# Two-layer trunk, convolution stage: two weight slabs split earlier, six taps moved from TensorE to VectorE

## What is computed

```
for i in range(2):
    x = x + 0.5 * swiglu_ffn(rms_norm(x, ffn1_norm[i]), ffn1_w_in[i], ffn1_w_out[i])
    xn = rms_norm(x, mix_norm[i])
    y = pool_conv_mixer(xn, ...) if i == 0 else sgu_mixer(xn, ...)
    x = x + y
    x = x + 0.5 * swiglu_ffn(rms_norm(x, ffn2_norm[i]), ffn2_w_in[i], ffn2_w_out[i])
out = rms_norm(x, final_norm)
```

```
a, gate = split(h)                      # 512 channels each
g = a * sigmoid(gate)
y = causal depthwise conv(g, width 31) + conv_b
return silu(layer_norm(y))              # mean and variance over the 512 channels
```

## Time and profile before

| | before |
|---|---|
| median of 3 runs | 940.22 us (940.21 to 940.26) |
| profiled execution, first to last instruction | 938.5 us |
| around that span, in the median | 1.7 us |
| PE busy | 927.6 us (99%) |
| DVE busy | 522.7 us (56%) |
| ACT busy | 411.9 us (44%) |
| mix0's convolution part, PE's first tap to the mean | 239.7 to 267.0 us |

### The profile page before, as it was taken

One profiled execution on the slowest core, in us unless ns is written; L12 is line 12 of the kernel. 1 busy time (PEld: TensorE's weight loads), 2 busy tenths in 40 slices (PEclk: granted clock), 3 DMA queues, 4 the chain that ended last, 5 costly groups with the idle time before them and its releaser, 6 DMA issues.

```text
span 938.5 us, 15299 instructions
## 1 busy us (share of the span) xinstructions
PE 927.6 (99%) x6505; PEld 872.2 (93%) x6505; DVE 522.7 (56%) x464; ACT 411.9 (44%) x413; POOL 26.7 (3%) x44
## 2 busy tenths in 40 slices
PE   8999999999999999999999999999999999999997
PEld 7999999989989999999999999999999899999995
DVE  5765545446967665455547444554478475454533
ACT  6453334326744544333435344334364265343322
POOL 1500000000000000000000000000010000000000
PEclk9999999999999999999999999999999999999999
DMA  8985555523512875676518656556184277556501
GB/s 264 310 270 179 179 179 201 196 75 120 172 46 101 303 241 180 217 236 202 179 45 278 217 179 213 184 197 190 46 288 161 90 242 263 185 177 209 196 7 45
DMA packets 124213, 170.36 MB, mean 182 GB/s; under 512 B 2773, under 2 KB 108777, under 8 KB 124168
## 3 DMA queue, kind: packets, MB, share of 16 engines
q1 hardware_dynamic: 124168, 169.69, 54.1%
HBM read 168.63 MB, written 1.05 MB: 181 GB/s over the span
## 4 chain that ended last, share of the span: by engine, by line
PE 96%; issue 1%; DVE 1%; DMA 1%; ACT 1%; POOL 0%; SPq 0%; POOLq 0%; ACTq 0%; DVEq 0%
PE ub L894 10%; PE ub L896 10%; PE ub L895 10%; PE ga L894 10%; PE ga L896 10%; PE ga L895 10%; PE acc L894 10%; PE acc L895 10%; PE acc L896 10%; PE ga L1093 1%; PE tp L955 1%; DMA raw<-in_ffn_w_in_dram 1%; PE ub L1093 1%; PE tp L1180 0%; DVE w_lo L607 0%
## 5 line engine op out<-in xcount | busy, mean ns | idle before, releaser
L607 DVE TENSOR_TENSOR w_lo<-raw,w_hi 128x2048 fp32r<-128x2048 f32 (+1 forms) x154 | 352.1, 2295 | 246.3 <-ACT w_hi L410 246.1
L410 ACT ACTIVATE w_hi<-raw 128x2048 fp32r<-128x2048 f32 (+1 forms) x154 | 292.1, 1902 | 91.9 <-PE acc L896 61.5
L894 PE MATMUL ub<-xn_hi,w_hi 128*128 128x256 f32 x688 | 195.1, 284 | 0.0
L894 PE MATMUL ga<-xn_hi,w_hi 128*128 128x256 f32 x688 | 194.8, 283 | 0.2 <-ACT sgh L455 0.2
L896 PE MATMUL ub<-xn_hi,w_lo 128*128 128x256 f32 x688 | 194.7, 283 | 0.0
L895 PE MATMUL ub<-xn_lo,w_hi 128*128 128x256 f32 x688 | 194.7, 283 | 0.0
L896 PE MATMUL ga<-xn_hi,w_lo 128*128 128x256 f32 x688 | 194.7, 283 | 0.0
L895 PE MATMUL ga<-xn_lo,w_hi 128*128 128x256 f32 x688 | 194.7, 283 | 0.0
L894 PE MATMUL acc<-w_hi,act_hi 128*128 128x512 f32 x416 | 163.6, 393 | 0.0
L895 PE MATMUL acc<-w_lo,act_hi 128*128 128x512 f32 x416 | 162.3, 390 | 0.0
L896 PE MATMUL acc<-w_hi,act_lo 128*128 128x512 f32 x416 | 161.9, 389 | 0.0
(11 more groups left out here) (130 smaller groups left out, 766.0 us busy)
## 6 DMA issues: line engine op xcount, KB each, us to landing
raw<-in_ffn_w_in_dram SPq DMA_DIRECT2D x88, 1024.0 KB, 5.1
raw<-in_ffn_w_out_dram SPq DMA_DIRECT2D x44, 1024.0 KB, 5.0
raw<-in_sgu_w_in_dram SPq DMA_DIRECT2D x8, 1024.0 KB, 5.3
raw<-in_ab_w_in_dram SPq DMA_DIRECT2D x6, 1024.0 KB, 4.9
raw<-in_ab_w_out_dram SPq DMA_DIRECT2D x4, 1024.0 KB, 4.8
raw<-in_sgu_w_out_dram SPq DMA_DIRECT2D x4, 1024.0 KB, 7.1
gain<-in_ffn_norm_dram SPq DMA_DIRECT2D x4, 512.0 KB, 5.8
xres<-in_x_dram SPq DMA_DIRECT2D x2, 512.0 KB, 6.3
```

The source lines that it names most:

```text
L410: act.activation(w_hi[:, n % RING, o:], raw[:, n % RAW, o:], ACT.Copy).then_inc(hi_split, 1)
L607: dve.tensor_tensor(w_lo[:, n % RING, o:], raw[:, n % RAW, o:], w_hi[:, n % RING, o:].bitcast(F32), ALU.subtract).then_inc(lo_split, 1)
L894: pe.matmul(dst, s_hi, m_hi, start=start, stop=False)
```

## The change

`SHARED` falls from 16 to 10, so TensorE does the last 10 taps of tile 2 and not 16, ACT builds 41 diagonals and not 47, and DVE does 21 taps of tile 2 and not 15. ACT splits slab b+6 ahead of the first 16 diagonals. DVE splits slabs b+5 and b+6 ahead of the second gate product; the split after q = 8 goes, the ones after q = 12 and 16 are again slabs b+7 and b+8.

```diff
-        SHARED = 16
+        SHARED = 10
         pe_taps = [(CT - 1, q) for q in range(TAPS)] + [(CT - 2, q) for q in range(TAPS - SHARED, TAPS)]
...
                     gate(b + 2, f + 1, ACT.Sigmoid)
+                    split_to(b + 6)
                     act.wait_ge(cols_ready, 1)
                     build_taps(0, DIAGS)
-                    split_to(b + 6)
...
+                    split_to(b + 6)
                     product(b + 3, f + 1, out=conv_in[:, 2:4, LEAD:])
-                    split_to(b + 5)
                     dve.wait_ge(ub_free, f + 2)
                     for q in range(5, TAPS):
 
                         for c in (0, 2, 1) if q - 5 < TAPS - SHARED else (0, 1):
                             tap(c)
 
-                        if q in (8, 12, 16):
-                            split_to(b + 6 + (q - 8) // 4)
+                        if q in (12, 16):
+                            split_to(b + 7 + (q - 12) // 4)
```

## The result

| | before | after |
|---|---|---|
| median of 21 runs | 940.12 us (939.93 to 940.26) | 942.58 us (940.90 to 943.93) |
| ratio of the mean times | | 1.0023, 95% interval 1.0016 to 1.0029 |
| profiled execution, span | 938.5 us | 941.0 us |

The changed kernel is slower, by 0.23% in the mean of its runs and by 2.46 us (0.26%) in the median, and outside my range of 940.5 to 941.8. The runs of after don't scatter, they fall in three groups: 7 runs at 940.90 to 941.09, 11 at 942.34 to 942.79, and 3 at 943.67 to 943.93. The runs of before form one group, 0.3 us wide. The first group of after is my forecast of 941.08; two thirds of the runs are not in it.

What follows compares the result with a forecast made beforehand. TensorE was taken to bound the stage, VectorE 1.2 us behind. Six taps save TensorE 2.59 us, but it must wait for VectorE, so the mean starts 0.86 us later: 940.22 + 0.86 = 941.08 us, range 940.5 to 941.8.

Steps and rivals of the forecast that it cites:

- Parts 1 and 2: Convolution stage: six taps leave TensorE, saving 2.59 us at 0.432 each, and cost VectorE 2.38 us at 0.396 each.
- Parts 3 and 4: Before the second product: early splits leave VectorE 4.2 us less loaded; ScalarE's first 16 diagonals start 1.9 us later, costing nothing.
- The wait at L802: Middle of VectorE's taps: it waits 3.6 us for ScalarE's unmoved high part, so the addition ends at 267.75, 1.92 us later.
- Rival B: TensorE's pause before the mean: its clock falls, costing 1.8 us, at worst twice that; 942.9 to 944.7 us, chance 0.08.
- The new hole is shorter: TensorE's pause before the mean: 3.3 us, against the 4.6 us from stop to clock fall at the kernel's end.

Runs made afterwards that it cites:

- SHARED 8: The changed kernel with SHARED = 8 in place of 10, two more taps on VectorE: 944.40 us median, five runs at 943.47 to 944.49.

## Why the prediction was wrong

Point by point:

- **Parts 1 and 2, the price of a tap on either engine: right.** With the wait out of the way 2.59 us came back, and 22 taps on VectorE took the forecast 8.71 us from start to start (258.51 to 267.22).
- **Parts 3 and 4, the moved splits: right.** Product at 228.43 (228.6 forecast), first tap at 229.15 (229.3), the splits alone change nothing (940.09 against 940.10 us).
- **The wait at L802: right.** 3.53 us (3.6 forecast), addition at 267.22 (267.34), pause 3.30 us (3.3). It holds for the part of the time that it was about: 7 of the 21 runs lie at 940.90 to 941.09, my 941.08.
- **Rival B, the clock: this is the step that failed.** Its price was right (1.8 us forecast and at worst 3.6; measured 1.7 and 2.8), though it rested on the lengths of the start-up records alone (275 ns in the median, up to 581 ns): for the clock over them the windows of before read 1.00. Its chance was not right: 0.08, and 16 of 23 runs of the changed kernel had it. So the forecast put the clock's cost behind the pause at nothing, and in the median run it was 1.6 us. The failing sentence is "The new hole is shorter". I had one event, the fall 4.6 us after the last matmul at the kernel's end, and took the 4.6 us for the length that a pause must have. It was only the delay from stop to fall. In the profiled run of after the fall came 4.45 us after the stop, when TensorE had been at work again for 1.15 us: starting again did not call it off, and so it was in four of the five profiles with a fall. In the fifth it came after 2.1 us, inside the pause. At the kernel's end itself the delay lies anywhere from 2.2 to 4.6 us. So one delay bounds neither how long a pause is safe nor when the fall comes; in the experiments, pauses of 2.3 us were already caught in 4 of 11 runs. What decides from run to run whether and when the clock falls, in one and the same pause, stays open.
- **The median.** I made a time of one mechanism and treated the rival as a tail. With 2 runs of 3 in it, the rival is the median: 941.0 + 1.6 = 942.6.

The Trainium skill's passage that I weighed (page "TensorE: Matmul & The Clock Gate", section "HAM oscillation — how this bites in real kernels": bursts separated by waits of some 3 to 5 us each began at the lower clock) described this case better than my reading of the earlier trace rows. The runs here agree with it at 3.75 and 4.95 us (10 of 10) and in most runs at 3.3 us (16 of 23), and go below it: 10 falls in 22 runs with pauses of 2.3 and 2.5 us.

## What to carry to other kernels

Moving work off the bounding engine pays only if the other engine's whole list moves with it: look for a wait in the middle of that list which today is met with little to spare (here 0.5 us, and so in no view of waits), since it eats whatever is gained ahead of it, and everything added behind it is late in full. A new pause of the matmul engine is to be priced twice, once for its length and once for the clock: here pauses of 2.3 us and more cost another 1.4 to 2.9 us behind them, in a share of the runs that grew with the pause over the whole table (neighbouring rows of it are too close to tell apart). Filling the pause with matmuls of no use, or better, moving the small work with the wait a few steps back, takes that away; runs in separate groups a microsecond or two apart are the sign to look at the granted clock.

## What the runs showed of the hardware

The granted clock can fall when the engine has already been busy again for 1.15 us, and it can fall 2.1 us into a pause of 3.3 us; both happened at the same place of the same program. It stayed low for 3.4 us in four profiles (two of the changed kernel, one each of the six taps alone and of SHARED 8) and for 6.8 us in a fifth, a run of the changed kernel's uppermost group, where 5.7 us of that were work; the upper two times of the changed kernel are 941.0 us plus half of the work at the lower clock. A pause of 1.66 us brought it on in none of 11 runs, one of 0.52 us in none of 11.
